# Residual products in three token blocks, weights streamed three times

## What is computed

```python
return x + o.reshape(B, T, V_DIM) @ w_out, new_conv, S      # 2048 x 1024
return x + (jax.nn.silu(h @ w1) * (h @ w3)) @ w2            # 2816 x 1024
x = x + o @ p['swa_w_o'][ib]                                # 1024 x 1024
```

## Time and profile before

| | |
|---|---|
| Median of 3 runs | 5019.57 us (5018.34 to 5022.19) |
| The profiled execution | 5027.78 us, its span 5026.2 us |
| PE busy with matmuls | 4490.8 us, 89% of the span |
| DVE, ACT, POOL busy | 1931.8, 1593.8, 979.0 us (38%, 32%, 19%) |
| DMA traffic | 563.57 MB, mean 112 GB/s |
| mixout, ffndown, attout | from 1305.7, 2123.8 and 3054.0 us on |

### The profile page before, as it was taken

The page is one execution under the profiler, slowest core; times in us unless marked ns, Lnnn a source line. Parts: engine busy times, 40 slices in busy tenths (PEclk is TensorE's granted clock), DMA queues, the critical chain, the costliest instruction groups (busy, mean ns, idle before and its releaser), DMA issues. The chain is left out here.

```text
span 5026.2 us, 93860 instructions
## 1 busy us (share of the span) xinstructions
PE 4490.8 (89%) x38127; PEld 4226.5 (84%) x38127; DVE 1931.8 (38%) x3018; ACT 1593.8 (32%) x2919; POOL 979.0 (19%) x863
## 2 busy tenths in 40 slices
PE   8999979999796999899778888499999999999993
PEld 7899978888695999899545667399999999999993
DVE  5665136666312000011112222244545455455554
ACT  6631223333222000022101222233434444444442
POOL 3344124444231232133100002200000000000001
PEclk9999989999998999999888557699999999999997
DMA  2222244443331222134120001465657666676675
GB/s 95 77 91 95 78 115 103 111 95 81 107 115 51 64 68 72 54 118 124 43 48 1 0 0 52 124 173 149 170 159 189 166 183 177 173 198 181 177 206 201
DMA packets 930563, 563.57 MB, mean 112 GB/s; under 512 B 137520, under 2 KB 890496, under 8 KB 930320
## 3 DMA queue, kind: packets, MB, share of 16 engines
q1 hardware_dynamic: 907808, 486.33, 34.9%
q10 hardware_dynamic: 12336, 46.60, 2.9%
q0 software_dynamic: 10176, 27.19, 2.0%
HBM read 481.79 MB, written 77.93 MB: 111 GB/s over the span
## 5 line engine op out<-in xcount | busy, mean ns | idle before, releaser
L2276 DVE TENSOR_TENSOR experts_w_lo<-experts_raw,experts_w_hi 128x1024 fp32r<-128x1024 f32 x352 | 416.1, 1222 | 159.6 <-ACT experts_w_hi L2208 159.6
L209 PE MATMUL experts_pa<-experts_hx,experts_w_hi 128*128 128x272 f32 (+5 forms) x1408 | 410.6, 292 | 8.4 <-DVE experts_w_lo L2276 8.4
L209 PE MATMUL experts_pd<-experts_hid,experts_w_hi 128*128 128x272 f32 (+5 forms) x1408 | 410.9, 292 | 0.0
L210 PE MATMUL experts_pa<-experts_hx,experts_w_hi 128*128 128x272 f32 (+5 forms) x1408 | 410.2, 291 | 0.0
L211 PE MATMUL experts_pa<-experts_hx,experts_w_lo 128*128 128x272 f32 (+5 forms) x1408 | 409.5, 291 | 0.0
L209 PE MATMUL experts_pb<-experts_hx,experts_w_hi 128*128 128x272 f32 (+5 forms) x1408 | 407.9, 290 | 1.2 <-DVE experts_w_lo L2276 1.2
L210 PE MATMUL experts_pb<-experts_hx,experts_w_hi 128*128 128x272 f32 (+5 forms) x1408 | 408.5, 290 | 0.0
L211 PE MATMUL experts_pd<-experts_hid,experts_w_lo 128*128 128x272 f32 (+5 forms) x1408 | 408.2, 290 | 0.0
L211 PE MATMUL experts_pb<-experts_hx,experts_w_lo 128*128 128x272 f32 (+5 forms) x1408 | 407.9, 290 | 0.0
L210 PE MATMUL experts_pd<-experts_hid,experts_w_hi 128*128 128x272 f32 (+5 forms) x1408 | 407.8, 290 | 0.0
L209 PE MATMUL front_pm<-front_hT,front_w_hi 128*128 128x384 f32 (+1 forms) x1152 | 388.8, 337 | 19.2 <-POOL front_w_lo L471 16.3
(11 more groups left out here) (403 smaller groups left out, 11070.1 us busy)
## 6 DMA issues: line engine op xcount, KB each, us to landing
experts_raw<-in_moe_w SPq DMA_DIRECT2D x352, 512.0 KB, 4.8
experts_raw<-in_moe_w SPq DMA_DIRECT2D x128, 704.0 KB, 5.6
projected<-front_out SPq DMA_DIRECT2D x48, 544.0 KB, 3.5
front_w<-in_w_proj ACTq DMA_DIRECT2D x48, 512.0 KB, 3.5
ffnup_w<-in_ffn_w SPq DMA_DIRECT2D x44, 512.0 KB, 5.1
ffndown_w<-in_ffn_w SPq DMA_DIRECT2D x32, 704.0 KB, 4.5
mixout_w<-in_gdn_w_out SPq DMA_DIRECT2D x32, 512.0 KB, 3.8
delta_kkq<-projected SPq DMA_DIRECT2D x102, 128.0 KB, 2.9
```

What stands on the lines that cost most here:

```text
L209: pe.matmul(out, as_r(w_hi), as_r(x_hi), start=first, stop=False)
L210: pe.matmul(out, as_r(w_hi), as_r(x_lo), start=False, stop=False)
L2276: dve.tensor_tensor(as_r(w_lo[:, x, 0:KD, :]), raw[:, x, 0:KD, :], w_hi[:, x, 0:KD, :], ALU.subtract).then_inc(split[x], 1)
```

## The change

The tokens are worked on in the three blocks `BLK` of 384, 384 and 320 that other stages use already, instead of two halves of two blocks of 272. One block fits one PSUM bank, so a row takes 3 matmuls in a pass, 9 over the three blocks. All weights are streamed once per block, so three times. The ring of four slots becomes one slot per row (`raw` with `kt` rows of 384), and SP's order changes: after the first two strips of weights of a block it issues all rows of the next block, each when the row in its slot has been split, and then the other strips. The first two strips of a block are issued outside the loop.

```diff
--- before.py
+++ after.py
@@ -1328,27 +1328,21 @@
                         dve.tensor_tensor(rest, srest, pm[:, 1, 2, 0:320], ALU.mult).then_inc(gated, 1)
 
 
-HALF = TOK // 2
-HBLK = [(0, HALF // 2), (HALF // 2, HALF // 2)]
-RAW = 4
-
-
 def add_product_stage(nc, m, name, src, kt, load, parts=1, resident=False):
 
-
-
     xT = m["xT"]
-    PAIRS, kh = KD // 2, kt // 2
+    PAIRS, kh, NB = KD // 2, kt // 2, len(BLK)
+    WIDE = BLK[0][1]
     with Stage(nc, name) as st:
         w, w_hi, w_lo = (st.sb(n, [P, 2, kh, P]) for n in ("w", "w_hi", "w_lo"))
-        x = st.sb("x", [P, 2, kt, HALF])
-        raw = None if resident else st.sb("raw", [P, RAW, HALF])
-        pm = st.ps("pm", [P, 2, 2, 512])
+        x = st.sb("x", [P, 2, kt, WIDE])
+        raw = None if resident else st.sb("raw", [P, kt, WIDE])
+        pm = st.ps("pm", [P, 2, 512])
         two = lambda n: [st.sem(f"{n}{u}") for u in range(2)]
         w_loaded, w_rounded, w_split, w_used, added = (two(n) for n in ("w_loaded", "w_rounded", "w_split", "w_used", "tile_added"))
-        src_loaded = [st.sem(f"src_loaded{r}") for r in range(RAW)]
+        src_loaded = [] if resident else [st.sem(f"src_loaded{r}") for r in range(kt)]
         src_rounded, src_split, k_used = st.sem("src_rounded"), st.sem("src_split"), st.sem("k_used")
-        piece = lambda h, k: src[:, k, h * HALF:(h + 1) * HALF] if resident else raw[:, (h * kt + k) % RAW, :]
+        piece = lambda h, k: src[:, k, BLK[h][0]:sum(BLK[h])] if resident else raw[:, k, 0:BLK[h][1]]
         with st.block() as block:
             @block.sync
             def _(sp):
@@ -1359,28 +1353,34 @@
                             sp.dma_start(to, frm).then_inc(w_loaded[p], 16)
 
                 def source(h):
+                    c, n = BLK[h]
                     for k in range(0 if resident else kt):
-                        q = h * kt + k
-                        if q >= RAW:
-                            sp.wait_ge(src_split, PRE + q - RAW + 1)
-                        sp.dma_start(raw[:, q % RAW, :], src[k, :, h * HALF:(h + 1) * HALF]).then_inc(src_loaded[q % RAW], 16)
-
-                for h in range(2):
-                    weights(h, 0)
-                    source(h)
-                    with sp.Fori(1, KD) as i:
+                        if h:
+                            sp.wait_ge(src_split, PRE + (h - 1) * kt + k + 1)
+                        sp.dma_start(raw[:, k, 0:n], src[k, :, c:c + n]).then_inc(src_loaded[k], 16)
+
+                weights(0, 0)
+                source(0)
+                for h in range(NB):
+                    if h:
+                        weights(h, 0)
+                    weights(h, 1)
+                    if h + 1 < NB:
+                        source(h + 1)
+                    with sp.Fori(2, KD) as i:
                         weights(h, i)
 
             @block.gpsimd
             def _(pool):
-                with pool.Fori(0, 2 * KD) as t:
+                with pool.Fori(0, NB * KD) as t:
                     for p in range(2):
                         pool.wait_ge(w_rounded[p], PRE + t + 1)
                         pool.tensor_tensor(as_r(w_lo[:, p, :, :]), w[:, p, :, :], w_hi[:, p, :, :], ALU.subtract).then_inc(w_split[p], 1)
 
             @block.tensor
             def _(pe):
-                for h in range(2):
+                for h in range(NB):
+                    n = BLK[h][1]
                     with pe.Fori(0, PAIRS) as i:
                         for u in range(2):
                             pe.wait_ge(added[u], PRE + PAIRS * h + i)
@@ -1389,9 +1389,7 @@
                                 if k % kh == 0:
                                     pe.wait_ge(w_split[p], PRE + KD * h + 2 * i + u + 1)
                                 pe.wait_ge(src_split, PRE + h * kt + k + 1)
-                                for b, (c, n) in enumerate(HBLK):
-                                    last = split_product(pe, pm[:, u, b, 0:n], w_hi[:, p, k % kh, :], w_lo[:, p, k % kh, :], x[:, 0, k, c:c + n], x[:, 1, k, c:c + n],
-                                                         k == 0, k == kt - 1)
+                                last = split_product(pe, pm[:, u, 0:n], w_hi[:, p, k % kh, :], w_lo[:, p, k % kh, :], x[:, 0, k, 0:n], x[:, 1, k, 0:n], k == 0, k == kt - 1)
                                 last.then_inc(w_used[p] if k % kh == kh - 1 else k_used, 1)
 
             @block.scalar
@@ -1401,18 +1399,17 @@
                     act.wait_ge(w_used[p], PRE + t)
                     act.activation(as_r(w_hi[:, p, :, :]), w[:, p, :, :], ACT.Copy).then_inc(w_rounded[p], 1)
 
-                for h in range(2):
+                for h in range(NB):
                     for k in range(kt):
-                        q = h * kt + k
                         if k % kh == 0:
                             weights(KD * h, k // kh)
                         if not resident:
-                            act.wait_ge(src_loaded[q % RAW], PRE + 16 * (q // RAW + 1))
+                            act.wait_ge(src_loaded[k], PRE + 16 * (h + 1))
                         if h and k % kh < kh - 1:
-                            act.wait_ge(k_used, PRE + (kt - 2) * (KD - 1) + k - k // kh + 1)
+                            act.wait_ge(k_used, PRE + (kt - 2) * (KD * h - 1) + k - k // kh + 1)
                         elif h:
-                            act.wait_ge(w_used[k // kh], PRE + KD)
-                        act.activation(as_r(x[:, 0, k, :]), piece(h, k), ACT.Copy).then_inc(src_rounded, 1)
+                            act.wait_ge(w_used[k // kh], PRE + KD * h)
+                        act.activation(as_r(x[:, 0, k, 0:BLK[h][1]]), piece(h, k), ACT.Copy).then_inc(src_rounded, 1)
                     with act.Fori(1, KD) as i:
                         for p in range(2):
                             weights(KD * h + i, p)
@@ -1422,24 +1419,23 @@
                 def split(h):
                     for k in range(kt):
                         dve.wait_ge(src_rounded, PRE + h * kt + k + 1)
-                        dve.tensor_tensor(as_r(x[:, 1, k, :]), piece(h, k), x[:, 0, k, :], ALU.subtract).then_inc(src_split, 1)
+                        dve.tensor_tensor(as_r(x[:, 1, k, 0:BLK[h][1]]), piece(h, k), x[:, 0, k, 0:BLK[h][1]], ALU.subtract).then_inc(src_split, 1)
 
                 def add(h, i, u):
                     dve.wait_ge(w_used[1], PRE + KD * h + 2 * i + u + 1)
-                    to = xT[:, bass.ds(2 * i + u, 1), h * HALF:(h + 1) * HALF].rearrange("p o (b t) -> p (o b) t", b=2)
-                    dve.tensor_tensor(to, to, pm[:, u, :, 0:HALF // 2], ALU.add).then_inc(added[u], 1)
+                    c, n = BLK[h]
+                    to = xT[:, bass.ds(2 * i + u, 1), c:c + n].rearrange("p o t -> p (o t)")
+                    dve.tensor_tensor(to, to, pm[:, u, 0:n], ALU.add).then_inc(added[u], 1)
 
                 split(0)
-                with dve.Fori(0, PAIRS - 1) as i:
-                    add(0, i, 0)
-                    add(0, i, 1)
-                add(0, PAIRS - 1, 0)
-                split(1)
-                add(0, PAIRS - 1, 1)
-                with dve.Fori(0, PAIRS) as i:
-                    add(1, i, 0)
-                    add(1, i, 1)
-
+                for h in range(NB):
+                    with dve.Fori(0, PAIRS - 1) as i:
+                        add(h, i, 0)
+                        add(h, i, 1)
+                    add(h, PAIRS - 1, 0)
+                    if h + 1 < NB:
+                        split(h + 1)
+                    add(h, PAIRS - 1, 1)
 
 
 K_CACHE = WINDOW + PROMPT
```

## The result

The changed kernel takes 5056.95 us (median of 4 runs, 5051.85 to 5062.71) beside 5020.88 us for the kernel before on the same chip: ratio 1.0072, 95% interval 1.0055 to 1.0089. The profiled execution took 5062.71 us, span 5061.2 against 5026.2 before.

A forecast was written before the change was run, and what follows sets the result against it. PE was taken to set the pace in mixout and ffndown, the weight round in attout. Mixout -2.8, ffndown -14.0 and attout +52.3 gave +35.5 us, so 5055 us, 0.7% slower; forecast 5040 to 5070, range 5035 to 5080.

The forecast's parts named there:

- Attout: Attout stage: the weight round, not PE, stays the bound over 24 passes instead of 16; +52.3 us.
- The eight added rounds: Attout: eight more weight rounds of 6.92 us each, not shortened by PE's shorter passes; +55.4 us.
- the rounds written outside the loop: Attout: weight rounds outside SP's loop take 6.47 us, 0.45 less, six instead of two; 1.8 us off.
- The lower bound of +33: Attout: least added time, from 24 rounds of 6.0 us against 16 of 6.92.
- The rule on issuing: Attout: skill page calls DMA initiation usually small; prediction counted SP's 0.599 us per issue, eight times a round, instead.
- Matmuls: Mixout and ffndown: wider matmuls, 0.178 us for 384 columns, save PE 1.6 and 2.2 us, almost nothing.
- The first block: Start of mixout and ffndown: loads and the wait before the third tile; overheads of 13.8 and 18.4 us.
- Changes of block and the narrow block: Block changes lose 5.0 and 4.5 us in mixout, 6.6 and 6.5 in ffndown; narrow blocks 5.0 and 1.1.
- SP not the bound: Attout rival: weight round hidden under a wide pass of 4.28 us; -28 us in all, 4992 us, chance 0.05.
- Changes as dear as before: Mixout and ffndown rival: block changes cost today's half starts, 10.5 and 16.3 us each; +31, 5086 us, chance 0.12.
- Free changes: Mixout and ffndown rival: block changes cost nothing; -22.6 us, 5032 us, chance 0.08.
- A falling clock in attout: Attout rival: PE idles and drops to 1.2 GHz, wide pass 7.65 us; +12 us, 5067 us, chance 0.07.

The follow-up runs named there:

- e3: Changed kernel, but attout loads each half of its weights by one DMA instead of four; attout's stretch 129.55 us against 168.13.
- e7: Changed kernel, but in attout each half of the weights has two buffers, same number of DMAs; attout 156.12 us, ratio 1.0039 to the kernel before.
- e5: Changed kernel's three blocks, but rows come through the old ring of four, asked for at their own block's start; ratio 1.0191 to the kernel before.
- e4: Changed kernel, but in mixout and ffndown POOL subtracts only the first row of each weight half; ratio 0.9996 to the kernel before.

## Why the prediction was right, step by step

The time was 5056.95 us for 5055, but part of that closeness is luck: mixout came 0.6 us longer than its sum, ffndown 2.4 longer, attout 3.6 shorter. Inside the stages, too, terms offset each other: mixout's start came 2.7 us late, and its 14 wide passes after it saved 3.4 us.

- *Attout.* 168.1 us for 171.7. The eight added rounds are there, 6.88 us each for 6.92. The term that was mis-sized is the rounds written outside the loop: 3102.82 - 3096.60 = 6.22 us for 6.47, six of them, 1.5 us of the 3.6; the rest is not traced. The reason given was half right. I built the 6.92 as one chain through the single buffer, with SP's arithmetic in it; the two-buffer run shows that SP's eight issues alone make 6.2 on the mean, 0.5 us less than the changed kernel's mean of 6.7. Neither the waits for the DMA nor my sum could tell the two apart; SP's own waits could have. The lower bound of +33, from rounds of 6.0, left SP's arithmetic out and was lower than any run with eight DMAs a pass came.
- *The rule on issuing.* The Trainium skill, "DMA: Bandwidth & Descriptors", section "Issuing engines are not separate DMA queues", says that issuing from several engines saves only the time to initiate a DMA, usually small beside the DMA. In the run with two buffers that time is the bound: 0.599 us for each issue, 6.2 us a pass with what lies between. Moving half of it to a second queue took attout in halves from 118 and 122 to 109 us, but together with a second buffer, so that run does not test the rule.
- *Matmuls.* A wide pass in mixout takes 8.32 us for 8.56 ((1446.28 - 1429.64) / 2) and the narrow block a round of 7.78 for 7.5 ((1527.25 - 1480.56) / 6), by the additions below. Ffnup's 0.178 us for 384 columns was too long a price: here it is 0.173. So the wide passes gave 16 x 0.24 = 3.8 us more than the sum has in mixout, and with 11.44 for 11.77 us 5.3 more in ffndown: small, but not the nothing that I forecast.

```profile
1429.64 0.56 DVE L1428 TENSOR_TENSOR xT<-xT,mixout_pm 128x384 f32 x1 [7.79 <-PE mixout_pm L211]
...
1446.28 0.56 DVE L1428 TENSOR_TENSOR xT<-xT,mixout_pm 128x384 f32 x1 [7.78 <-PE mixout_pm L211]
...
1480.56 0.49 DVE L1428 TENSOR_TENSOR xT<-xT,mixout_pm 128x320 f32 x1 [7.98 <-PE mixout_pm L211]
...
1527.25 0.49 DVE L1428 TENSOR_TENSOR xT<-xT,mixout_pm 128x320 f32<-128x320 f32 x1 [7.40 <-PE mixout_pm L211]
```

- *The first block.* The third tiles start 33.6 and 43.8 us after the stages' first issue, for 30.9 and 41.9. In ffndown the weights behind the rows are rounded at 39.1 us (2161.82 - 2122.72) for a landing 37.2 us in, and from there to PE it takes 4.66 us for 4.6. So the term at fault is the landing, 1.9 us too early. The rate was right: 329 GB/s over the stretch for 333, with the DMA engines busy throughout, so SP's 11.47 us of issuing is not the reason. What the 2161 adds up to is twice 17.3 us, the first two strips and 44 rows; the third tile's own first piece, 0.72 MB or 2.2 us at that rate, fits what is missing. I also put PE's wait there at 1.9 us; it was 5.3, since PE's own two passes ended earlier than thought.
- *Changes of block and the narrow block.* I put them at 14.5 us in mixout and 14.2 in ffndown. Shortening POOL took 15.1 and 18.7 us away, 2.8 and 2.5 of them at the start, so 12.3 and 16.2 at the changes and in the narrow block. The price was about right; its direction was half right. I had POOL's pass hold up DVE's splits, and at three of the four changes PE does wait for a split first; the dearest gap, 6.08 us, was DVE's chain of splits holding up POOL. The Trainium skill, "SBUF — State Buffer", section "🔬 SBUF: two separate sides", calls the pair of ports that both use an exclusive lock: whoever comes first has it for a whole instruction, the other blocks fully. The trace agrees that one blocks the other, and shows more than one instruction's wait: 9.3 us instead of 3.2, with splits of 0.48 to 0.54 us in front.
- *The rivals.* SP not the bound: excluded by e3 and e7. Changes as dear as before: excluded, as that would be 1.3% and 0.7% was measured; e5, where the rows do come no earlier, took 1.9%. Free changes: excluded by the 6.08 us above; e4 shows what is left when POOL's part is taken out. A falling clock in attout: 0.94 against 0.95, no part of the time. Where the clock does count is a place that the sum has no term for, mixout and ffndown behind PE's long waits: 2.8 us at ffndown's second change alone.

## What to carry to other kernels

A tiling that streams the weights once more costs one round of the weights' path for each tile, wherever that path (issue, landing, rounding, subtraction, per buffer) is longer than PE's pass; read it from who waits for the DMA, and then ask whether the issuing queue itself ever waits. When one change bundles two things, here loading ahead and more blocks, price them apart: the first alone was worth 0.8 to 0.9%; the second took 21.8 us of it back in mixout and ffndown and cost 48.7 more in attout. A wait of PE can cost more than its length: look at the granted clock behind it. Moving a wait in one queue, as the order of weights and rows, only helps if the work behind it fits under a pass.

## What was not expected of the hardware

One of attout's four DMAs for a piece occupies SP for 0.60 us, and 0.78 with what lies between two (149.1 / 191 in the run with two buffers), so the eight of a pass keep it busy for 6.2 us. DVE subtracts 128 x 1408 fp32 in 1.626 us where POOL takes 3.22. Successive short DVE operations can hold back a POOL operation several times its length: 3.2 became 9.3 us, 2.4 became 8.7 (mixout in halves), while a split of 0.54 took 3.5 us at most.
